# MLA's last two gate units by K tile, and two output units grown between the pieces of the last head

## What is computed

```
u = h @ w_in
c_q, c_kv, k_rope, z = jnp.split(u, ...)               # 384, 256, 32, 1024 features
q = rmsnorm_2(c_q, q_norm) @ w_q_b                     # 16 heads of 64 + 32 (rope)
kv = rmsnorm_2(c_kv, kv_norm) @ w_kv_b                 # 16 heads of 64 keys + 64 values
prob = softmax(block-causal(q k^T * scale))            # q, k with rope parts
o = prob @ v
return (o * jax.nn.silu(z)) @ w_out
...
x = x + y
gate = jax.nn.sigmoid(rmsnorm_2(x) @ ple_gate[i])
x = x + gate * (p[i] @ ple_proj[i])
```

## Time and profile before

| | us |
|---|---|
| median of 3 runs | 2151.73 (2150.18 to 2152.19) |
| profiled execution | 2151.38 |
| its span | 2149.6 |
| PE busy | 2040.2 |
| DVE, POOL, ACT busy | 1038.6, 1025.3, 674.9 |

### The profile page before, as it was taken

How to read it: one execution, slowest core, us unless ns; L and a number is a source line. 1 busy time by engine, 2 the same in 40 slices (tenths; PEclk the granted TensorE clock), 3 DMA queues, 4 the chain that set the end, 5 groups by cost and what they waited for, 6 DMA issues and landing times.

```text
span 2149.6 us, 26333 instructions
## 1 busy us (share of the span) xinstructions
PE 2040.2 (95%) x9488; PEld 1649.8 (77%) x9488; DVE 1038.6 (48%) x1212; ACT 674.9 (31%) x1083; POOL 1025.3 (48%) x651
## 2 busy tenths in 40 slices
PE   4999999988999999999999999999899999989997
PEld 3777776877888878878887888887677777768785
DVE  6645554636442212212212248332787788864446
ACT  3335554231121000000000024112466666660322
POOL 1545555521743543543453347333555566553364
PEclk9999999997999999999999999999899999999998
DMA  3100000112211111211111123111000000001123
GB/s 140 51 21 21 17 13 20 49 40 88 98 59 49 60 58 49 69 59 49 49 61 49 46 64 112 39 49 41 30 21 20 20 20 20 30 30 49 39 69 117
DMA packets 31660, 106.65 MB, mean 50 GB/s; under 512 B 3458, under 2 KB 3650, under 8 KB 31604
## 3 DMA queue, kind: packets, MB, share of 16 engines
q1 hardware_dynamic: 27520, 96.14, 13.6%
q10 hardware_dynamic: 4084, 9.74, 1.3%
HBM read 101.51 MB, written 4.26 MB: 49 GB/s over the span
## 4 chain that ended last, share of the span: by engine, by line
PE 84%; DVE 7%; ACT 4%; issue 4%; POOL 1%; ACTq 0%; DVEq 0%; DMA 0%; POOLq 0%
PE ps L228 56%; PE ps L374 8%; PE ps L245 3%; PE ps L258 3%; PE ps L618 2%; PE ps L606 2%; PE ps L619 2%; DVE mx L719 1%; PE ps L625 1%; PE ps L605 1%; PE ps L604 1%; ACT mla_p_hi L665 1%; PE ps L650 1%; PE ps L648 1%; DVE S_all L1297 1%
## 5 line engine op out<-in xcount | busy, mean ns | idle before, releaser
L1964 POOL TENSOR_TENSOR w_hi<-w_raw,zero 128x1024 fp32r<-128x1024 f32 (+2 forms) x173 | 320.3, 1851 | 790.8 <-PE ps L228 580.6
L1966 POOL TENSOR_TENSOR w_lo<-w_raw,w_hi 128x1024 fp32r<-128x1024 f32 (+2 forms) x173 | 407.3, 2355 | 13.6
L228 PE MATMUL ps<-h_hi,w_lo 128*128 128x512 f32 x1328 | 335.1, 395 | 5.3 <-DVE x L505 5.1
L228 PE MATMUL ps<-h_hi,w_hi 128*128 128x512 f32 x1328 | 328.0, 389 | 0.0
L228 PE MATMUL ps<-h_lo,w_hi 128*128 128x512 f32 x1216 | 300.6, 389 | 0.0
L228 PEld LDWEIGHTS ps<-h_hi,w_lo 128*128 128x128 f32 x1328 | 249.5, 189 | 60.1 <-issue 9.1
L228 PEld LDWEIGHTS ps<-h_hi,w_hi 128*128 128x128 f32 x1328 | 249.3, 188 | 51.7
L674 POOL TENSOR_TENSOR probs_lo<-probs,mla_p_hi 128x512 fp32r<-128x512 f32 x192 | 191.1, 1015 | 169.0 <-ACT probs L667 167.1
L228 PEld LDWEIGHTS ps<-h_lo,w_hi 128*128 128x128 f32 x1216 | 228.7, 188 | 47.8
L719 DVE TENSOR_REDUCE mx<-ps 128x1 f32<-128x128 f32 (+1 forms) x192 | 141.0, 755 | 79.4 <-PE ps L650 44.3
L674 POOL TENSOR_TENSOR probs_lo<-probs,fox_p_hi 128x512 fp32r<-128x512 f32 (+1 forms) x96 | 95.3, 1010 | 107.8 <-ACT probs L667 107.8
(11 more groups left out here) (351 smaller groups left out, 3675.3 us busy)
## 6 DMA issues: line engine op xcount, KB each, us to landing
w_raw<-in_wpack SPq DMA_DIRECT2D x173, 512.0 KB, 3.3
x<-in_xT ACTq DMA_DIRECT2D x16, 512.0 KB, 8.2
out<-result SPq DMA_DIRECT2D x8, 512.0 KB, 2.9
p_raw<-in_pT ACTq DMA_DIRECT2D x1, 1024.0 KB, 4.9
pos_i<-in_pos SPq DMA_DIRECT2D x1, 512.0 KB, 6.3
const_stage<-in_consts SPq DMA_DIRECT2D x1, 404.0 KB, 3.2
vec<-in_vecs SPq DMA_DIRECT2D x1, 284.0 KB, 5.4
mla_q_hi<-c_neg ACTq DMA_DIRECT2D x16, 4.0 KB
```

Source lines behind the costliest of these rows:

```text
L228: last = nc.tensor.matmul(dst[:, half, :], w[slot][:, kt, :], a[:, i, t], start=(n == 0), stop=(n == total - 1))
L1964: nc.gpsimd.tensor_tensor(w_hi[s][:, kts, :], raw[s][:, kts, :], no_change[:, kts, :], ALU.add).then_inc(w_hi_done, 1)
L1966: nc.gpsimd.tensor_tensor(w_lo[s][:, kts, :], raw[s][:, kts, :], w_hi[s][:, kts, :].bitcast(F32), ALU.subtract)\
```

## The change

At the opening, gate units 6 and 7 are made together, K tile by K tile, into PSUM banks 4 to 7. After each K tile a new semaphore `h_free` lets ACT copy the hi tile that goes to its place; the hi and lo tiles of c_q and c_kv are laid out so that tile k covers h's K tile k, and the heads' buffers cover K tiles 5 to 7. The norms' spreads and sums stand two units earlier. k_rope's copies now wait for the last gate unit.

At the closing, units U_MO and U_MO+1 are made together: K tiles 0 to 6 behind pieces 2 to 8 of the last head, K tile 7 after it. ACT copies mix tiles 0 to 2 behind pieces 8 to 10 of head 14 (its loop gives its last turn away as unrolled code), tiles 3 to 6 behind pieces 0 to 3 of head 15. POOL splits U_MO+1 before the last head's pieces.

```diff
-        ckv_hi, ckv_lo = at("ckv_hi", R_H + 24576, [P, 2, T], F32R), at("ckv_lo", R_H + 32768, [P, 2, T], F32R)
+        ckv_hi, ckv_lo = at("ckv_hi", R_H + 12288, [P, 2, T], F32R), at("ckv_lo", R_H + 45056, [P, 2, T], F32R)
...
+        Z_BANKS = (pjA, pjB) * (DT // 2 - 1) + (PS[:, 4:6, :], PS[:, 6:8, :])
...
-            between = {1: spread_q, 3: sum_kv, 5: spread_kv}
-            for i in range(DT):
+            between = {0: spread_q, 1: sum_kv, 3: spread_kv}
+            for i in range(DT - 2):
...
+            NKV.wait(pe, "h", 2)
+            for i in (DT - 2, DT - 1):
+                pe.wait_ge(w_split, U_Z + i + 3)
+            for kt in range(DT):
+                for i in (DT - 2, DT - 1):
+                    for half in range(2):
+                        for n, (w, a) in enumerate(((w_lo, h_hi), (w_hi, h_lo), (w_hi, h_hi))):
+                            last = nc.tensor.matmul(Z_BANKS[i][:, half, :], w[(U_Z + i) % 2][:, kt, :], a[:, kt, cols(half)],
+                                                    start=(kt == 0 and n == 0), stop=(kt == DT - 1 and n == 2))
+                    if kt == DT - 1:
+                        last.then_inc(unit_done, 1)
+                if kt < DT - 1:
+                    last.then_inc(h_free, 1)
...
-            act.wait_ge(unit_done, U_Z + DT + 2)
+                silu(i)
             for s, n, k0, hi in ((NQ, 3, 0, cq_hi), (NKV, 2, 3, ckv_hi)):
                 s.wait(act, "h", n)
                 for k in range(n):
+                    act.wait_ge(h_free, k0 + k + 1)
                     nc.scalar.activation(hi[:, k, :], u5[:, k0 + k, :], ACT.Copy).then_inc(s["hi"], 1)
+            silu(6)
+            silu(7)
...
             act.wait_ge(kr_step, 4)
+            act.wait_ge(unit_done, U_Z + DT + 2)
...
+            if isinstance(n, int) and n == MLA_H - 1:
+                todo.update({8: lambda: out_hi_act(act, 0), 9: lambda: out_hi_act(act, 1), 10: lambda: out_hi_act(act, 2)})
...
+        MO_BEHIND = {g: g - 2 for g in range(2, 2 + DT - 1)}
+
+        def out_hi_act(act, k):
+            act.wait_ge(mla.norm_done, 4 * k + 4)
+            if k >= 5:
+                act.wait_ge(mla.pv_done, (MLA_H - 1) * N_PIECES + 4)
+            mix_hi_act(k, m2_hi)
+
+        def out_part_pe(pe, kt):
+            pe.wait_ge(m2_lo, kt + 1)
+            for u, dst in ((U_MO, pjA), (U_MO + 1, pjB)):
+                for half in range(2):
+                    for n, (w, a) in enumerate(((w_lo, h_hi), (w_hi, mix_lo), (w_hi, h_hi))):
+                        last = nc.tensor.matmul(dst[:, half, :], w[u % 2][:, kt, :], a[:, kt, cols(half)], start=(kt == 0 and n == 0),
+                                                stop=(kt == DT - 1 and n == 2))
+                if kt == DT - 1:
+                    last.then_inc(unit_done, 1)
...
+                if A is mla:
+                    split(U_MO + 1, (U_MO + 1) % 2, (U_MO + 1) // 2 * 16 + 16)
...
+            for k in range(4):
+                mix_lo_dve(dve, k, k, m2_hi, m2_lo)
             norm_whole_dve(dve, mla, MLA_H - 1, 1, 0, MLA_H // 2 - 1, True)
-            for k in range(2):
+            for k in range(4, DT - 1):
                 mix_lo_dve(dve, k, k, m2_hi, m2_lo)
             norm_whole_dve(dve, mla, MLA_H - 1, 1, 1, MLA_H // 2 - 1, True)
-            for k in range(2, DT - 1):
-                mix_lo_dve(dve, k, k, m2_hi, m2_lo)
             mix_lo_dve(dve, DT - 1, DT - 1, m2_hi, m2_lo)
...
-            last_pe(pe, mla)
-            project_tiles(pe, ((U_MO, pjA),), range(DT), h_hi, mix_lo, lambda i: pe.wait_ge(m2_lo, i + 1))
-            pe.wait_ge(w_split, U_MO + 1 + 3)
-            project(pe, (U_MO + 1) % 2, range(DT), h_hi, mix_lo, pjB)
+            last_pe(pe, mla, lambda g: out_behind_pe(pe, g))
+            out_part_pe(pe, DT - 1)
```

More of the change, by code:

```diff
@@ L578, in max_width, with buffers @@
             return w, i // 4 * HALF + w
[L580 to L583, removed]
+        def buffers(k, qk_at, klo_at, vaug_at, vlo_at, phi_at):
+            q_hi = [at(f"{k}_q_hi{b}", qk_at[b], [P, T], F32R) for b in range(2)]
+            q_lo = [at(f"{k}_q_lo{b}", qk_at[b] + 4096, [P, T], F32R) for b in range(2)]
+            k_hi = [at(f"{k}_k_hi{b}", qk_at[b] + 8192, [P, T], F32R) for b in range(2)]
             k_lo = [at(f"{k}_k_lo{b}", klo_at + 4096 * b, [P, T], F32R) for b in range(2)]
@@ L780, in maxima @@
                         pe.wait_ge(mla_constants, 6)
+                        pe.wait_ge(z_read, DT)
                 for i in MAX_AFTER.get(g, ()):
@@ L794, in step_pe, with last_pe @@
                     maxima(g)
-        def last_pe(pe, A):
+        def last_pe(pe, A, after=()):
             pe.wait_ge(A.row_in[1], 16 * (A.heads // 2))
@@ L799, in last_pe @@
                 score_pe(pe, A, A.heads - 1, 1, g)
-            attend_pe(pe, A, A.heads - 1, 1)
+            attend_pe(pe, A, A.heads - 1, 1, after)
         def step_act(act, A, n, b, turn, prepare):
@@ L814, in step_act, with last_act @@
             max_row_act(act, A, n, b, turn)
-        def last_act(act, A, split=None):
+        def last_act(act, A, after=lambda g: None):
             for g in range(N_PIECES):
@@ L820, in last_act @@
                     rough_act(act, A, A.heads - 1, 0)
-                if split is not None and g >= N_PIECES - 2:
-                    act.wait_ge(A.norm_done, 2 * (A.heads - 2))
-                    split(g - (N_PIECES - 2))
+                after(g)
             rough_act(act, A, A.heads - 1, 1)
-            if split is not None:
-                for k in range(2, DT - 1):
-                    split(k)
         def step_dve(dve, A, n, b, turn, prepare, tile0, gate):
@@ L841, in step_dve, with steps @@
                 norm_whole_dve(dve, A, prev, 1 - b, 1, tile, gate)
-        def steps(eng, A, step):
+        def steps(eng, A, step, unrolled=0):
             for b in range(2):
                 step(b, b, 0)
-            with eng.Fori(1, A.heads // 2) as turn:
+            with eng.Fori(1, A.heads // 2 - unrolled) as turn:
+                for b in range(2):
+                    step(turn * 2 + b, b, turn)
+            for turn in range(A.heads // 2 - unrolled, A.heads // 2):
                 for b in range(2):
@@ L1562, in mla_in_dve @@
                 norm_scaled(NKV, u5[:, 3 + k, :], u5[:, 3 + k, :], vec[:, V_KVN + k:V_KVN + k + 1]).then_inc(NKV["h"], 1)
-            z_scaled(6)
-            z_scaled(7)
+            z_scaled(4)
+            z_scaled(5)
             for s, n, k0, hi, lo in ((NQ, 3, 0, cq_hi, cq_lo), (NKV, 2, 3, ckv_hi, ckv_lo)):
-                s.wait(dve, "h", n)
                 for k in range(n):
@@ L1583, in mla_in_act, with silu @@
             square(NKV, 1, 4)
-            for i in range(DT):
-                if i == 4:
+            def silu(i):
+                act.wait_ge(z_read, i + 1)
+                nc.scalar.activation(mix[:, i, :], mix[:, i, :], ACT.Silu).then_inc(z_silu, 1)
+            for i in range(DT - 2):
+                if i == 2:
                     norm_root(act, NKV, KVL, DT)
@@ L1698, in mla_prepare_dve, with out_behind_pe, out_behind_act @@
             nc.vector.tensor_tensor(q_lo[b][CR, :], q[CR, :], q_hi[b][CR, :].bitcast(F32), ALU.subtract).then_inc(mla.lo_done, 1)
+        MO_BEHIND = {g: g - 2 for g in range(2, 2 + DT - 1)}
[13 more added lines that the diff above has]
+                    last.then_inc(unit_done, 1)
+        def out_behind_pe(pe, g):
+            if g == min(MO_BEHIND):
+                pe.wait_ge(w_split, U_MO + 1 + 3)
+                pe.wait_ge(mla.vaug_done, 2 * MLA_H)
+            if g in MO_BEHIND:
+                out_part_pe(pe, MO_BEHIND[g])
+        def out_behind_act(act, g):
+            if g < 4:
+                out_hi_act(act, 3 + g)
         m2_hi, m2_lo, mo_added = sem("mix2_hi"), sem("mix2_lo"), sem("mo_added")
@@ L2003, in _ @@
             heads(mla, U_HEAD, MLA_KTS)
-            units(U_HEAD + MLA_H + 1, N_UNITS)
+            units(U_MO + 2, N_UNITS)
         @block.scalar
```

30 lines of the change are left out of this document (14 added, 16 removed).

## The result

The changed kernel takes **2168.64 us** (median of 4 runs, 2167.75 to 2169.94), against 2150.95 us (4 runs, 2149.97 to 2152.19) for the kernel before on the same chip: a ratio of 1.008, with a 95% interval from 1.0068 to 1.0093. It is slower, by 17.7 us. The forecast was 2164.0 us in a range of 2157 to 2169, with 0.90 on slower: the side is right, the size 4.6 us short and close to the upper end.

A forecast was written before the change was run, and what follows sets the result against it. The prediction took PE, busy for 95% of the span, to bound the kernel. Opening +2.7 and closing +10.1 us on 2151.4 gave 2164.2, stated as 2164.0 us, range 2157 to 2169.

The forecast's parts named there:

- The opening: From the gate's last units to head 0's rope: the rope starts at 1513.5 instead of 1510.78, +2.7 us.
- The two stalls: At the opening, PE waits for POOL's weight splits: about 4.5 us before the gate's pair, 3.05 us before head 0.
- the term of 1.7 us for half clock: At the opening, a half-clock stretch of some 3.4 us behind a stall costs half of that, 1.7 us.
- The copies in head 14: Three hi copies on ACT behind exponentials 8 to 10 make the last head start later: +1.65 us.
- The attention with two units in it: Last head with 84 output-projection matmuls behind pieces 2 to 8, waits vanishing there: 36.2 us.
- The end of the head: Ahead of K tile 7, PE stands from the head's last matmul until the last lo tile: 6.6 us.
- Unit 2's start after the end of the attention: At the closing, norm 4.2 us, then 11.5 us until DVE's addition, later than the split, ends the wait.
- the long half clock: Behind the new stalls at opening and closing, half clock lasts long: 5.3 + 11.9 us, giving 2168.6 us.
- Rival (a): At the new stalls the clock does not fall: 0 + 8.4 us, 2159.8 us; chance 0.15.
- Rival (b): Half clock lasts long at opening and closing: 5.3 + 11.9 us, 2168.6 us; chance 0.15.
- Rival (c): No measurable change: p_raw's chain and ACT's copies stay off the path, the clock holds: 2154.8 us; chance 0.06.
- rival (d): Faster: weights already split when a pair begins or ends, so no opening stall: -5.7 us, 2145.7 us; chance 0.04.

The follow-up runs named there:

- x_warm: Kernel before with only the change's opening, plus 20 unread matmuls in the 4.5 us stall ahead of the gate's pair: 2151.99 us, 1.0003.
- x_copies: Changed kernel without the three hi copies in head 14 and the unrolled turn; all seven copies stand behind pieces 0 to 6 of the last head: 2164.74 us, 1.0061.
- x_lolate: Changed kernel with DVE's first four lo tiles held back until POOL has made the first low part: 2165.88 us, 1.0068.
- x_clock: Changed kernel with 27 unread matmuls ahead of K tile 7 and 16 behind it at the closing: 2168.53 us, 1.0085.
- x_praw: Changed kernel with ACT's DMA of p_raw issued before its wait for the last head instead of after its hi copy: 2165.97 us, 1.0072.
- x_lag: Kernel before with the change's opening reordered: gate units 6 and 7 alternate in halves of four K tiles, unit 7 lagging: 2147.99 us, 0.9984.
- x_best: Kernel before with x_lag's opening, a closing with only one unit behind the last head's pieces, and k_rope's copies ahead of the last silu: 2138.26 us, 0.9937.
- x_wait: Kernel before with one wait added: gate unit 6 also waits for unit 7's weights: 2154.71 us, 1.0017.

## Why the forecast was right on the side and short on the size

**The opening: +2.7 forecast, 4.0 found** (4.5 in the rope's start, 0.5 of which the trace already shows at the gate's first unit, 1395.38 for 1394.86). The two stalls came out as forecast: 4.54 us for 4.5, 3.2 for 3.05, each behind POOL's split, since a slot is free only when its unit is done. What failed is the term of 1.7 us for half clock: it lasted 4.9 us, to 1486.5, and the pair took 24.37 instead of 23.5; x_warm puts the price at 2.3 us or more. The 18 query matmuls took 5.97 us, 5.8 forecast. DVE's two lo tiles took 4.03 us, not 3.20, beside POOL's casts, and ended only just inside the queries.

**The copies in head 14: +1.65 forecast, 0.9 found** (x_copies). The sum passed nearly all of exponential 11's 1.8 us on to the last head; about half arrived. Where the rest was absorbed I did not follow.

**The attention with two units in it: 36.2 us forecast, 39.4 found** (1908.37 to 1947.75). This is the largest term, and the one whose step was wrong: "ACT and POOL need some 1.2 us per piece, PE now about 4, so waits vanish there". Waits over 0.3 us did vanish behind pieces 2 to 8, but at piece 0 the lo tiles, which the sum had as free work on DVE, stretched POOL's low part by 2.7 us. That is 1.8 us of waiting on PE and 1.1 of half clock behind it; x_lolate gives 2.8 us back, and its 36.2 us are the forecast's. The trace of before had the effect in small, behind the 0.85 us wait of the earlier trace rows:

```profile
1921.07 1.16 POOL L674 TENSOR_TENSOR probs_lo<-probs,mla_p_hi 128x128 fp32r<-128x128 f32 x1 [0.47 <-ACT probs L667]
```

That low part started 0.4 us after a mix_lo of DVE (1920.69); the one of the same size before it, at 1909.36, took 0.45 us. The prediction lists this wait and does not ask what made it.

**The end of the head: 6.6 us forecast, 6.62 found**, with nothing beside it, as the trace of before let one count.

**Unit 2's start after the end of the attention: 15.7 us forecast, 16.0 found.** The number was right and the releaser only half: the forecast named DVE's addition, and the split, forecast 5.8 or 7.0 us behind the last lo tile, ended 9.3 behind it (1963.64 less 1954.32), stretched beside p_lo, and so with the addition to 0.1 us. In x_clock the addition alone holds unit 2, in x_praw the split alone. Half clock behind it was 2.2 us (67.51 for 65.3), not 1.7.

**The sum.** The misses are +1.3 (opening), -0.7 (copies), +3.2 (attention), +0.3 (unit 2's start) and +0.5 (half clock behind it), and 0.5 of an earlier offset: 5.1 of the 5.2 us between 2164.2 and the profiled 2169.4. The earlier offset stays open; the pair starts at 1481.64 here and at 1480.68 in x_praw, whose code is the same up to there, so traces scatter by as much. That the time still lies inside the range owes something to luck: its upper end was set by the long half clock, not by the contention that carried the time there. Rival (a), the clock holding, is refuted by the windows. Rival (b), long half clock, gave the right total (2168.6) for a third of its reason: half clock was longer than I took it, but the contention made up the larger part, and no rival had that. Rival (c) fails by the two stalls, and rival (d), faster, by the earlier trace rows as argued; x_lag and x_best are what it would have taken. What was not separated is the unrolled turn of ACT from the copies in it; both together cost 0.9 us.

## What to carry to other kernels

Two units made side by side share both their ends: with two weight slots, the second unit's split can't start before the unit ahead of the pair is done, and the next unit's can't before the pair is. Let one lag the other by half a unit and the same early release of tiles comes without either stall. And before work is counted as free on an engine that idles, look at what else runs at that moment and might wait for it: here four small DVE operations cost 2.8 us on PE, and holding them for one operation took it away.

## What the runs showed of the hardware

POOL and DVE get in each other's way when both read two tiles of SBUF, and the one that starts second pays. In four places of these traces it ended by some 0.14 us less than its own length after the first had ended, as if it had waited:

- A low part of 128x512 takes 1.28 us alone. In the changed kernel it started during DVE's four lo tiles, took 4.00 us and ended 1.14 us after them (1915.22, 1914.08); the lo tiles kept their pace (4.61 us for four).
- w_lo of unit 2 takes 2.35 us alone. It started 0.44 us after p_lo, took 4.28 and ended 2.22 us after it (1963.64, 1961.42).
- In x_clock w_lo was first and took 2.41 us. p_lo, 2.29 alone, took 3.68 and ended 2.15 us after w_lo.
- The w_hi behind them, 1.89 us alone, started during p_lo, took 3.94 and ended 1.75 us after it.

The Trainium skill, "GPSIMD Engine Reference", section "1. Specifications", says that GpSimd's SBUF interfaces are shared with VectorE, with contention for DVE instructions that have two SBUF inputs. The traces agree: the DVE operations in the pairs above read two tiles of SBUF, while the addition x, which reads one from PSUM, took 1.15 us in x_clock although it started beside the 3.94 us w_hi.

Half clock did not last equally long behind stalls, nor longest behind the longest: in the kernel before 3.4 us behind the 4.77 us stall of the earlier trace rows and 6.4 behind the 3.11 us one of the earlier trace rows, in the changed kernel 4.9 behind the 4.54 us stall ahead of the pair. The price of a stall on PE, idle time and clock together, was 4.5 us for 2.8 us of standing in x_wait's trace (3.6 between the medians).
